# HGRN states with the heads of a pair taking turns on TensorE, a finer order of its steps, and the output stage's first loads in the joining stage

## The chip, the core and the metric

One core of a Trainium2 chip runs the whole kernel. Its engines are TensorE (PE, its weight loads are shown apart as PEld), VectorE (DVE), ScalarE (ACT), GpSimd (POOL) and SyncE (SP), which here only issues transfers. The metric is the device time of one launch in microseconds (us). The kernel before takes 4038.7 us (median of three runs, 4037.71 to 4042.99).

## The reference

One layer of a two-branch sequence mixer with an MLP, on 2048 latent tokens and 256 context tokens of width 1024, all in float32:

```python
h = modulate(rms_norm(x), shift, scale)
p = h @ w_in                        # columns for both head groups
oa = gated_delta(p)                 # 8 heads of 64, forward and backward summed
ob = hgrn2(p)                       # 8 heads of 64, tokens in column-major order of a 32 x 64 grid
ya = head_rms(oa, gdn_g) * silu(ga)
yb = from_col_major(head_rms(ob, hgrn_g)) * sigmoid(gb)
x = x + gate1 * (concat(ya, yb) @ w_out)
x = x + gate2 * (relu(modulate(rms_norm(x)) @ w1) ** 2 @ w2)
out = rms_norm(x)
```

HGRN2 in chunks: each chunk of 128 tokens has a state S (64 x 64 for each head and direction), S_t = f_t S_(t-1) + delta_t, and the output of a chunk is q_dec @ S of the chunk ahead of it, plus what comes from inside the chunk.

## The kernel before

The program is a row of stages with a barrier between them: `phase_front`, `phase_project`, `phase_gdn` (the delta heads), `phase_hgrn` (context, chunks, states), `phase_merge` and `phase_out`. The change touches the last three: the states, the joining stage and the output stage.

**`phase_hgrn_states`.** The chunk stage has left in SBUF, for each of the 16 chunks and 8 heads, the state increment `e.delta` (both directions, one in each half of the partitions), and the part of the output from inside the chunks, `e.oi`. In DRAM lie the decayed queries `e.sqd` (2 MB for a pair of heads) and the gates `e.sgb`. The stage works on four pairs of heads, `a`:

- `scan` (DVE, L2242): the recurrence over 16 chunks, one instruction for a head and chunk, each waiting by `scanned` for the one of the chunk before. It runs in two halves of four heads (`HB` = 4): `scan(0)` ahead of all, `scan(1)` behind `add(0)`.
- `order(h)` (ACT, L2207 and L2208): copies a head's states into `st`, two instructions; `st` holds four heads.
- `outputs(a)` (PE, L2170): for each head of the pair 16 products of the states (128 x 64) with 128 columns of queries, head 0 into partitions 0 to 63 of PSUM `ps`, then head 1 into partitions 64 to 127. It waits for the pair's queries (`q_in`), for `o_sum` of the pair before (`ps` is single) and for `ordered`.
- `add(a)` (DVE, L2250) sums `ps` and `e.oi` into `o`, `square(a)` (ACT, L2214) squares it, `sums(a)` (PE, L2179) sums over the head's channels, `roots(a)` (ACT, L2220) and `inverse(a)` (DVE, L2254, a reciprocal) give one factor for each token and head in `rt`, `spreads(a)` (PE, L2189, four blocks of 512 tokens) spreads it over the partitions into one of three buffers `bc`, and `scale(a)` (DVE, L2264, four blocks) multiplies. `gate` (POOL for the first three pairs, DVE for the last, L2153) multiplies by the gate, and the result is stored to `e.sy`.
- The SP queue, in order: queries and gates of pairs 0 and 1; for pair 2 a wait for `outputs(0)`, its queries, a wait for `gate(0)`, its gates, the store of pair 0; for pair 3 the same, one pair on. So the queries of pair 3 stand behind the wait for `gate(0)` and behind the gates of pair 2 and the store of pair 0.

Orders of the engines in this stage, written out by hand: PE outputs 0, outputs 1, sums 0, spreads 0, sums 1, spreads 1, outputs 3 and so on (with outputs 2 behind spreads 0); DVE scan 0, add 0, scan 1, inverse 0, add 1, scale 0, inverse 1, add 2 and so on; ACT order 0 to 3, square 0, order 4 and 5, roots 0, square 1, order 6 and 7, roots 1.

**`phase_merge`** joins the two directions of the delta heads, in four blocks `b` of 512 tokens with two sets of buffers: three loads of 1 MB (`y_of`, `y_ob`, `y_ga`), an add, squares, sums, roots, a scaling, 64 small transposing products, the gate, and a store to `e.sy`. The loads of block 2 wait until block 0 is through.

**`phase_out`** runs 288 units of 24 matmuls (128 x 128 by 128 x 512; each operand is split in a high and a low part, hence three products for each of 8 input tiles `k`). Units 0 to 7 are the output projection of block 0, 8 to 15 that of block 1, then the MLP. The weights of a unit (512 KB) go into one of two buffers `raw`, are split by ACT (`o_w_hi`, L2600) and DVE (`o_w_lo`, L2679) and used by PE (L2559 to L2561). The SP queue begins: weights 0, the joined input `yraw` of block 0 in four parts, weights 1, the residual `x1` of block 0 (2 MB), weights 2, `yraw` of block 1 (2 MB, behind the wait that all 8 tiles of block 0 are split), `x1` of block 1 (2 MB), weights 3, weights 4 and so on.

Of the kernel before, what the change touches and what calls it, by code (L numbers as in the profile page):

```python
# [28 lines left out]
P = 128  # L29
D = 1024  # L30
KT = D // P
# [2072 lines left out]
def phase_hgrn_states(nc, e):  # L2104

    NS = NC2 + NL2
    with ExitStack() as ctx:
# [19 lines left out]
        with nc.Block() as block:  # L2127
            @block.sync
            def _(sp):
                sp.dma_start(pick[:, :], e.consts[:, K_PICK, 0:NB * HEADS]).then_inc(const_in, 16)  # L2130
                sp.dma_start(spread[:, :, :], e.consts[0:HEADS, K_SPREAD:K_SPREAD + NB, :]).then_inc(const_in, 16)
                for a in range(PAIRS):
                    if a >= 2:
                        sp.wait_ge(full, 2 * (a - 1))
                    sp.dma_start(qd[:, a % 2], e.sqd[:, 2 * a:2 * a + 2, :]).then_inc(q_in[a % 2], 16)
                    if a >= 2:
                        sp.wait_ge(gated, a - 1)
                    sp.dma_start(gb[:, a % 2], e.sgb[a]).then_inc(g_in[a % 2], 16)
                    if a >= 2:
                        sp.dma_start(e.sy[PAIRS + a - 2], yb[:, a % 2]).then_inc(stored[a % 2], 16)  # L2140
                for a in range(PAIRS - 2, PAIRS):
                    if a == PAIRS - 1:
                        sp.wait_ge(gated_last, 1)
                    else:
                        sp.wait_ge(gated, a + 1)
                    sp.dma_start(e.sy[PAIRS + a], yb[:, a % 2]).then_inc(stored[a % 2], 16)
                for p in range(2):
                    sp.wait_ge(stored[p], 32)
# [12 lines left out]
            def _(pe):  # L2161
                def outputs(a):
# [3 lines left out]
                    for x in range(2):  # L2166
                        h = 2 * a + x
                        pe.wait_ge(ordered, 2 * (h + 1))
                        for c in range(NL2):
                            last = nc.tensor.matmul(ps[x * HD:x * HD + HD, c * C2:(c + 1) * C2], st[:, h % 4, c, :],  # L2170
                                                    qd[:, a % 2, x, c * C2:(c + 1) * C2], start=True, stop=True)
                        last.then_inc(full, 1)
# [19 lines left out]
                outputs(0)  # L2192
                for a in range(PAIRS):
                    if a == 0:
                        outputs(1)
                    sums(a)
                    spreads(a)
                    if 0 < a + 2 < PAIRS:
                        outputs(a + 2)

            @block.scalar
            def _(act):
                def order(h):
                    act.wait_ge(scanned, NL2 * HB * (h // HB) + (NL2 - 1) * HB + h % HB + 1)
                    if h >= 4:
                        act.wait_ge(full, h - 3)
# [20 lines left out]
                for a in range(PAIRS):  # L2227
                    square(a)
                    if a + 2 < PAIRS:
                        order(2 * a + 4)  # L2230
                        order(2 * a + 5)
                    roots(a)

            @block.vector
            def _(dve):
                def scan(g):
                    for t in range(1, 1 + NL2):
                        for x in range(HB):
                            h = HB * g + x
                            if t >= 2:  # L2240
                                dve.wait_ge(scanned, NL2 * HB * g + (t - 2) * HB + x + 1)
# [3 lines left out]
                def add(a):  # L2245
                    dve.wait_ge(full, 2 * (a + 1))
# [22 lines left out]
                scan(0)  # L2269
                for a in range(PAIRS):  # L2270
                    add(a)
                    if a == 0:
                        scan(1)
                    if a:
                        scale(a - 1)
                    inverse(a)
                scale(PAIRS - 1)
# [13 lines left out]
def phase_merge(nc, e):  # L2291

    G = TB // CH
    with ExitStack() as ctx:
# [12 lines left out]
        stored = [sem("y_st0"), sem("y_st1")]  # L2307
        added, squared, summed, root, inv, scaled, turned, gated = (
            sem("y_" + n) for n in ("add", "sq", "sum", "root", "inv", "scaled", "turned", "gated"))
        with nc.Block() as block:  # L2310
            @block.sync
            def _(sp):
                for b in range(NB):
# [6 lines left out]
                    sp.dma_start(ga[:, p], e.sga[:, :, b * TB:(b + 1) * TB].rearrange("a p t -> p a t")).then_inc(load[p], 16)  # L2320

# [53 lines left out]
def phase_out(nc, e):  # L2375

    FC = FF // D
    with ExitStack() as ctx:
# [9 lines left out]
        x1 = sb("o_x1", [P, 2, KT, TB])  # L2388
        yraw = sb("o_yraw", [P, KT, TB])
        raw = sb("o_raw", [P, 2, KT, P])  # L2390
# [8 lines left out]
        w_in, x_in, out_st = ([sem(n + "0"), sem(n + "1")] for n in ("w_in", "x_in", "out_st"))  # L2399
        y_in = [sem("y_in%d" % i) for i in range(4)]  # L2400
# [7 lines left out]

        units = []
# [61 lines left out]
        with nc.Block() as block:  # L2471
            @block.sync
            def _(sp):
# [8 lines left out]
                def y_load(b):  # L2482
                    if b:
                        sp.wait_ge(y_lo_ready, KT * b)
                    for i in range(4):
# [12 lines left out]

                weights(0)
                y_load(0)  # L2500
                weights(1)
                x_load(0)
# [37 lines left out]
            def _(pe):  # L2540
                def unit(i):
# [8 lines left out]
                    for k in range(KT):  # L2550
                        if s == 0:
                            if kind == "o":
                                pe.wait_ge(y_lo_ready, KT * b + k + 1)
# [5 lines left out]
                        nc.tensor.matmul(out, w_hi[:, i % 2, k, :], rhs[0][:, k, :], start=(k == 0), stop=False)  # L2559
                        nc.tensor.matmul(out, w_hi[:, i % 2, k, :], rhs[1][:, k, :], start=False, stop=False)  # L2560
                        last = nc.tensor.matmul(out, w_lo[:, i % 2, k, :], rhs[0][:, k, :], start=False, stop=(k == KT - 1))  # L2561
# [33 lines left out]
            def _(act):  # L2595
# [58 lines left out]
                for k in range(KT):  # L2654
# [21 lines left out]
            def _(dve):  # L2676
# [4 lines left out]
                def y_split(b, k):  # L2681
                    hi, lo = y_pair(b)
                    dve.wait_ge(y_hi_ready, KT * b + k + 1)
# [46 lines left out]
                for k in range(KT):  # L2730
                    y_split(0, k)
                for i in range(LAST):
# [20 lines left out]
                    if at_step(i, KT + 2) is not None:  # L2753
                        inverse(at_step(i, KT + 2))


def program(nc, a):
# [7 lines left out]
    with ExitStack() as ctx:  # L2765
# [37 lines left out]
        phase_merge(nc, e)  # L2803
        phase_out(nc, e)

# [17 lines left out]
```

## Time and profile before

| | |
|---|---|
| median of three runs | 4038.7 us |
| the profiled execution | 4046.5 us |
| its span, first to last instruction | 4044.7 us |
| PE busy | 3591.9 us (89%) |
| DVE, ACT, POOL busy | 45%, 38%, 22% |
| granted TensorE clock, mean | 0.925 |
| HGRN states | 2203.6 to 2327.7 us |
| joining stage | 2332.1 to 2419.0 us |
| output stage | 2419.4 us to the end |

The profile shows one execution. "Busy" is time in which an engine executes; the idle time ahead of an instruction is shown in brackets with what ended it. A row of a timeline gives start, duration and instruction; xN means N instructions in one row. A granted clock of 1.00 is TensorE at 2.4 GHz, 0.50 at 1.2 GHz. A stage is read from its own stretch of the trace, since the averages over the span mix stages with different limits.

### The profile page before, as it was taken

What the parts mean: (1) busy time and instruction counts of PE and PEld (TensorE: products, weight loads), DVE (VectorE), ACT (ScalarE), POOL (GpSimd) and SP (SyncE); (2) the same over time, 40 slices, a digit from 0 to 9 for tenths busy, and PEclk for the clock granted to TensorE, in tenths of its full rate; (3) what the DMA queues carried; (4) which work ended last, traced back from release to release, by engine and by line L of the source; (5) the groups of instructions that cost most, each with busy time, mean ns of one, the idle gap of its engine ahead of it and who ended that gap; (6) DMA issues with size and microseconds to landing.
All of it is one profiled execution on the core that took longest, in us unless ns stands there. A gap on an engine that the chain in (4) does not pass through costs nothing. (4 is left out here: it accounts for less than half of the span.)

```text
span 4044.7 us, 98792 instructions
## 1 busy us (share of the span) xinstructions
PE 3591.9 (89%) x42320; PEld 2982.7 (74%) x42320; DVE 1824.9 (45%) x2710; ACT 1526.2 (38%) x2048; POOL 894.5 (22%) x872
## 2 busy tenths in 40 slices
PE   6899999999788888858776729999999999999999
PEld 3677888888577777747666427888888888888887
DVE  5488302110155555545555545444543454435443
ACT  5566324432255555413334113333422343234223
POOL 0220233320245555325553102000100110011001
PEclk8899999999799999956776769999999999999999
DMA  6233434442233333243332255333343333333332
GB/s 250 76 82 60 97 101 141 136 138 66 88 109 104 108 105 109 87 117 97 97 84 86 94 196 158 115 99 117 108 124 99 94 115 116 98 98 111 99 95 88
DMA packets 599111, 441.14 MB, mean 109 GB/s; under 512 B 119948, under 2 KB 548304, under 8 KB 591576
## 3 DMA queue, kind: packets, MB, share of 16 engines
q1 hardware_dynamic: 574048, 408.20, 34.7%
q0 software_dynamic: 5632, 16.78, 1.4%
q10 hardware_dynamic: 19192, 12.65, 1.1%
q8 instruction: 190, 3.11, 0.3%
q14 instruction: 49, 0.40, 0.0%
HBM read 338.17 MB, written 99.39 MB: 108 GB/s over the span
## 5 line engine op out<-in xcount | busy, mean ns | idle before, releaser
L618 PE MATMUL p_pg<-h_hi,p_whi 128*128 128x512 f32 (+1 forms) x1384 | 531.3, 384 | 10.0 <-DVE p_wlo L847 10.0
L2600 ACT ACTIVATE o_w_hi<-o_raw 128x1024 fp32r<-128x1024 f32 x288 | 303.6, 1054 | 590.6 <-PE o_pg L2561 551.8
L618 PE MATMUL p_pg<-h_hi,p_wlo 128*128 128x512 f32 (+1 forms) x1384 | 519.2, 375 | 0.0
L618 PE MATMUL p_pg<-h_lo,p_whi 128*128 128x512 f32 (+1 forms) x1384 | 519.2, 375 | 0.0
L2559 PE MATMUL o_pg<-o_f_hi,o_w_hi 128*128 128x512 f32 x1088 | 424.8, 390 | 0.0
L2561 PE MATMUL o_pg<-o_f_hi,o_w_lo 128*128 128x512 f32 x1088 | 423.3, 389 | 0.0
L2560 PE MATMUL o_pg<-o_f_lo,o_w_hi 128*128 128x512 f32 x1088 | 423.3, 389 | 0.0
L2559 PE MATMUL o_pg<-o_h_hi,o_w_hi 128*128 128x512 f32 x1024 | 400.0, 391 | 1.7 <-DVE o_w_lo L2679 1.7
L2561 PE MATMUL o_pg<-o_h_hi,o_w_lo 128*128 128x512 f32 x1024 | 398.5, 389 | 0.0
L2560 PE MATMUL o_pg<-o_h_lo,o_w_hi 128*128 128x512 f32 x1024 | 398.4, 389 | 0.0
L2679 DVE TENSOR_TENSOR o_w_lo<-o_raw,o_w_hi 128x1024 fp32r<-128x1024 f32 x288 | 351.4, 1220 | 77.4 <-ACT o_w_hi L2600 77.3
L2534 POOL COPY o_rt<-o_sq 128x512 f32<-128x512 f32 x8 | 9.2, 1151 | 1389.2 <-ACT o_sq L2614 1389.2
L618 PEld LDWEIGHTS p_pg<-h_hi,p_whi 128*128 128x128 f32 x1384 | 262.4, 190 | 61.5 <-DVE p_wlo L847 10.3
L618 PEld LDWEIGHTS p_pg<-h_lo,p_whi 128*128 128x128 f32 x1384 | 262.3, 190 | 51.2 <-issue 5.5
L2695 DVE SCALAR_TENSOR_TENSOR o_x<-o_pg,mod,o_x 128x512 f32<-128x512 f32 x160 | 119.9, 750 | 397.3 <-PE o_pg L2561 392.7
L618 PEld LDWEIGHTS p_pg<-h_hi,p_wlo 128*128 128x128 f32 x1384 | 262.0, 189 | 46.9
L2701 DVE TENSOR_TENSOR o_rl<-o_rl 128x512 f32<-128x512 f32 x128 | 88.7, 693 | 393.8 <-ACT o_f_hi L2640 393.8
L2638 ACT ACTIVATE o_rl<-o_pg 128x512 f32<-128x512 f32 x128 | 76.5, 598 | 430.3 <-PE o_pg L2561 430.3
L2559 PEld LDWEIGHTS o_pg<-o_f_hi,o_w_hi 128*128 128x128 f32 x1088 | 204.2, 188 | 43.4 <-issue 0.7
L2560 PEld LDWEIGHTS o_pg<-o_f_lo,o_w_hi 128*128 128x128 f32 x1088 | 204.3, 188 | 42.8 <-issue 0.7
L2561 PEld LDWEIGHTS o_pg<-o_f_hi,o_w_lo 128*128 128x128 f32 x1088 | 204.2, 188 | 42.5
L826 ACT ACTIVATE p_y<-p_pg 128x512 f32<-128x512 f32 (+1 forms) x108 | 97.0, 898 | 361.1 <-PE p_pg L618 245.3
(310 smaller groups left out, 6909.6 us busy)
## 6 DMA issues: line engine op xcount, KB each, us to landing
o_raw<-in_w_mlp SPq DMA_DIRECT2D x256, 512.0 KB, 4.1
g_kqvb<-scr_kqv SPq DMA_DIRECT2D x72, 384.0 KB, 3.4
p_raw<-in_w_in SPq DMA_DIRECT2D x38, 512.0 KB, 5.9
g_kqa<-scr_kqv SPq DMA_DIRECT2D x72, 256.0 KB, 3.1
p_mw<-in_w_mod POOLq DMA_DIRECT2D x64, 256.0 KB, 3.1
o_raw<-in_w_out SPq DMA_DIRECT2D x32, 512.0 KB, 4.1
scr_kqv<-p_y SPq DMA_DIRECT2D x24, 576.0 KB, 5.7
scr_hf<-p_y SPq DMA_DIRECT2D x16, 576.0 KB, 5.5
```

The source lines that it names most:

```text
L618: last = nc.tensor.matmul(pg[0:m, bank, 0:n], w[:, q, k, 0:m], h[bank][:, k, :], start=(k == 0 and j == 0), stop=(k == KT - 1 and j == 2))
L826: last = nc.scalar.activation(put(yrow[u]), src, f)
L2534: nc.gpsimd.tensor_copy(rt[:, c % 3, :], sq[:, n % 3, :]).then_inc(sq_used, 1)
L2559: nc.tensor.matmul(out, w_hi[:, i % 2, k, :], rhs[0][:, k, :], start=(k == 0), stop=False)
L2560: nc.tensor.matmul(out, w_hi[:, i % 2, k, :], rhs[1][:, k, :], start=False, stop=False)
L2561: last = nc.tensor.matmul(out, w_lo[:, i % 2, k, :], rhs[0][:, k, :], start=False, stop=(k == KT - 1))
L2600: nc.scalar.activation(w_hi[:, i % 2], raw[:, i % 2], ACT.Copy).then_inc(w_hi_ready, 1)
L2638: nc.scalar.activation(rl[:, n % 3, :], pg[:, i % 4, :], ACT.Relu).then_inc(rectified, 1)
L2679: dve.tensor_tensor(w_lo[:, i % 2], raw[:, i % 2], w_hi[:, i % 2].bitcast(F32), ALU.subtract).then_inc(w_lo_ready, 1)
L2695: dve.scalar_tensor_tensor(x, pg[:, i % 4, :], e.mod[:, gate:gate + 1], x, ALU.mult, ALU.add).then_inc(added, 1)
L2701: dve.tensor_tensor(rl[:, n % 3, :], rl[:, n % 3, :], rl[:, n % 3, :], ALU.mult).then_inc(f_sq, 1)
```

## The change

In the states: `outputs(a)` now waits for both heads of the pair and issues, chunk by chunk, the product of head 0 and then that of head 1; `full` counts pairs. `scan` runs in four parts of two heads. The orders become: PE outputs 0, outputs 1, sums 0, outputs 2, spreads 0, sums 1, outputs 3, spreads 1, sums 2, sums 3, spreads 2, spreads 3; DVE scan 0, scan 1, add 0, scan 2, add 1, inverse 0, scan 3, scale 0, add 2, inverse 1, scale 1, add 3, inverse 2, scale 2, inverse 3, scale 3; ACT order 0 to 3, square 0, order 4 and 5, roots 0, square 1, order 6 and 7, roots 1, square 2 and so on. The SP queue keeps its order; its waits on `full` are recounted.

In the joining stage, SP issues behind the loads of block 1 also weights 0 and 1 of the output stage, the second half of `yraw` of block 0 (the HGRN part, 1 MB) and its `x1` (2 MB), 4 MB in all. The output stage then loads only the first half of `yraw` of block 0 ahead of weights 2, and takes the tiles of block 0 in the order 4 to 7, 0 to 3 (`FIRST`), in unit order, in the splits and in the waits. The buffers and semaphores of these loads are made in a new function around both stages. Left out below: the allocations that move there, and one of two alike loops over `FIRST`.

```diff
@@ -2131,7 +2131,7 @@
...
                     if a >= 2:
-                        sp.wait_ge(full, 2 * (a - 1))
+                        sp.wait_ge(full, a - 1)
@@ -2163,13 +2163,12 @@
...
                         pe.wait_ge(o_sum, a)
-                    for x in range(2):
-                        h = 2 * a + x
-                        pe.wait_ge(ordered, 2 * (h + 1))
-                        for c in range(NL2):
-                            last = nc.tensor.matmul(ps[x * HD:x * HD + HD, c * C2:(c + 1) * C2], st[:, h % 4, c, :],
+                    pe.wait_ge(ordered, 4 * (a + 1))
+                    for c in range(NL2):
+                        for x in range(2):
+                            last = nc.tensor.matmul(ps[x * HD:x * HD + HD, c * C2:(c + 1) * C2], st[:, (2 * a + x) % 4, c, :],
                                                     qd[:, a % 2, x, c * C2:(c + 1) * C2], start=True, stop=True)
-                        last.then_inc(full, 1)
+                    last.then_inc(full, 1)
@@ -2190,20 +2189,23 @@
...
                 outputs(0)
+                outputs(1)
+                sums(0)
                 for a in range(PAIRS):
-                    if a == 0:
-                        outputs(1)
-                    sums(a)
+                    if a + 2 < PAIRS:
+                        outputs(a + 2)
+                    if a + 2 >= PAIRS and a + 1 < PAIRS:
+                        sums(a + 1)
                     spreads(a)
-                    if 0 < a + 2 < PAIRS:
-                        outputs(a + 2)
+                    if a + 2 < PAIRS:
+                        sums(a + 1)
...
                 def order(h):
-                    act.wait_ge(scanned, NL2 * HB * (h // HB) + (NL2 - 1) * HB + h % HB + 1)
+                    act.wait_ge(scanned, 2 * NL2 * (h // 2 + 1) - 1 + h % 2)
                     if h >= 4:
-                        act.wait_ge(full, h - 3)
+                        act.wait_ge(full, h // 2 - 1)
@@ -2224,26 +2226,33 @@
...
                     order(h)
-                for a in range(PAIRS):
-                    square(a)
-                    if a + 2 < PAIRS:
-                        order(2 * a + 4)
-                        order(2 * a + 5)
-                    roots(a)
+                square(0)
+                order(4)
+                order(5)
+                roots(0)
+                square(1)
+                order(6)
+                order(7)
+                for a in range(1, PAIRS):
+                    if a + 1 < PAIRS:
+                        roots(a)
+                        square(a + 1)
+                    else:
+                        roots(a)
...
             def _(dve):
-                def scan(g):
+                def scan(a):
                     for t in range(1, 1 + NL2):
-                        for x in range(HB):
-                            h = HB * g + x
+                        for x in range(2):
+                            h = 2 * a + x
                             if t >= 2:
-                                dve.wait_ge(scanned, NL2 * HB * g + (t - 2) * HB + x + 1)
+                                dve.wait_ge(scanned, 2 * (NL2 * a + t - 2) + x + 1)
...
                 def add(a):
-                    dve.wait_ge(full, 2 * (a + 1))
+                    dve.wait_ge(full, a + 1)
@@ -2267,14 +2276,18 @@
...
                 scan(0)
+                scan(1)
+                add(0)
+                scan(2)
+                add(1)
+                inverse(0)
+                scan(3)
                 for a in range(PAIRS):
-                    add(a)
-                    if a == 0:
-                        scan(1)
-                    if a:
-                        scale(a - 1)
-                    inverse(a)
-                scale(PAIRS - 1)
+                    scale(a)
+                    if a + 2 < PAIRS:
+                        add(a + 2)
+                    if a + 1 < PAIRS:
+                        inverse(a + 1)
@@ -2305,6 +2318,7 @@
...
         stored = [sem("y_st0"), sem("y_st1")]
+        wo = e.w_out[0]
@@ -2318,6 +2332,13 @@
...
                     sp.dma_start(ga[:, p], e.sga[:, :, b * TB:(b + 1) * TB].rearrange("a p t -> p a t")).then_inc(load[p], 16)
+                    if b == 1:
+                        for i in range(2):
+                            sp.dma_start(e.o_raw[:, i], wo[:, i * P:(i + 1) * P].rearrange("(k p) c -> p k c", p=P)).then_inc(e.o_w_in[i], 16)
+                        for i in range(PAIRS // 2, PAIRS):
+                            sp.dma_start(e.o_yraw[:, 2 * i:2 * i + 2], e.sy[2 * i:2 * i + 2, :, 0:TB].rearrange("k p t -> p k t")
+                                         ).then_inc(e.o_y_in[i], 16)
+                        sp.dma_start(e.o_x1[:, 0], e.xT[:, :, 0:TB].rearrange("k p t -> p k t")).then_inc(e.o_x_in[0], 16)
@@ -2406,6 +2425,7 @@
...
+        FIRST = [*range(PAIRS, KT), *range(PAIRS)]
@@ -2479,10 +2499,10 @@
...
-                def y_load(b):
+                def y_load(b, quarters=range(4)):
...
                         sp.wait_ge(y_lo_ready, KT * b)
-                    for i in range(4):
+                    for i in quarters:
@@ -2496,10 +2516,7 @@
...
-                weights(0)
-                y_load(0)
-                weights(1)
-                x_load(0)
+                y_load(0, (0, 1))
@@ -2547,18 +2564,18 @@
...
                             pe.wait_ge(added, add_no[i - 3])
-                    for k in range(KT):
+                    for n, k in enumerate(FIRST if kind == "o" and b == 0 else range(KT)):
...
                             if kind == "o":
-                                pe.wait_ge(y_lo_ready, KT * b + k + 1)
+                                pe.wait_ge(y_lo_ready, KT * b + n + 1)
...
                         out = pg[:, i % 4, :]
-                        nc.tensor.matmul(out, w_hi[:, i % 2, k, :], rhs[0][:, k, :], start=(k == 0), stop=False)
+                        nc.tensor.matmul(out, w_hi[:, i % 2, k, :], rhs[0][:, k, :], start=(n == 0), stop=False)
                         nc.tensor.matmul(out, w_hi[:, i % 2, k, :], rhs[1][:, k, :], start=False, stop=False)
-                        last = nc.tensor.matmul(out, w_lo[:, i % 2, k, :], rhs[0][:, k, :], start=False, stop=(k == KT - 1))
+                        last = nc.tensor.matmul(out, w_lo[:, i % 2, k, :], rhs[0][:, k, :], start=False, stop=(n == KT - 1))
@@ -2651,7 +2668,7 @@
...
                 split(0)
-                for k in range(KT):
+                for k in FIRST:
@@ -2727,7 +2744,7 @@
...
                 split(0)
-                for k in range(KT):
+                for k in FIRST:
@@ -2754,6 +2771,20 @@
...
+def phase_tail(nc, e):
+    with ExitStack() as ctx:
+        def sem(n):
+            return ctx.enter_context(nc.semaphore("o_" + n))
...
+        e.o_x1 = ctx.enter_context(nc.sbuf_tensor("o_x1", [P, 2, KT, TB], F32))
+        e.o_yraw = ctx.enter_context(nc.sbuf_tensor("o_yraw", [P, KT, TB], F32))
+        e.o_raw = ctx.enter_context(nc.sbuf_tensor("o_raw", [P, 2, KT, P], F32))
+        e.o_w_in, e.o_x_in = ([sem(n + "0"), sem(n + "1")] for n in ("w_in", "x_in"))
+        e.o_y_in = [sem("y_in%d" % i) for i in range(4)]
+        phase_merge(nc, e)
+        phase_out(nc, e)
@@ -2800,9 +2831,8 @@
...
         phase_hgrn(nc, e)
-        phase_merge(nc, e)
-        phase_out(nc, e)
...
+        phase_tail(nc, e)
```

## Rows read from the trace of the kernel before

**Rows 1.** Stretches: us, busy PE, PEld, DVE, ACT, POOL (xcount), clock, DMA share, GB/s

```profile
2203.50:2327.80 124.30, 81.88 (x320) 48.52 (x320) 66.87 (x153) 28.46 (x26) 13.50 (x3) 0.68 0.33 127
...
2462.00:4044.00 1582.00, 1571.97 (x6986) 1300.17 (x6984) 722.58 (x818) 529.51 (x690) 99.38 (x61) 1.00 0.36 104
```

**Rows 2.** Timeline, first part of the HGRN states: start, duration, instruction, idle before

```profile
2203.59 12.62 DVE L2242 SCALAR_TENSOR_TENSOR h_delta<-h_delta,s_gs 128x64 f32<-128x64 f32 x64 [1.96 <-ACT s_gs L2224]
...
2215.66 1.06 ACT L2207 ACTIVATE s_st<-h_delta 64x1024 f32<-64x1024 f32 x1 [12.10 <-DVE h_delta L2242]
...
2217.94 9.31 PE L2170 MATMUL s_ps<-s_qd,s_st 128*64 128x128 f32 x64 [17.75 <-ACT s_st L2208]
...
2245.86 1.28 ACT L2220 ACT_TABLE_LOAD   x1
...
2247.87 3.34 DVE L2254 RECIPROCAL s_rt<-s_rt 8x512 f32<-8x512 f32 x1 [5.76 <-ACT s_rt L2220]
```

**Rows 3.** Timeline, last two pairs of the HGRN states

```profile
2282.76 9.35 PE L2170 MATMUL s_ps<-s_qd,s_st 128*64 128x128 f32 x64
...
2284.03 4.50 POOL L2153 TENSOR_TENSOR s_yb<-s_yb,s_gb 128x2048 f32<-128x2048 f32 x1 [19.86 <-DVE s_yb L2264]
...
2292.03 3.60 PE L2179 MATMUL s_pn<-s_sq,s_pick 128*8 128x512 f32 x8
...
2301.90 1.91 ACT L2214 ACTIVATE s_sq<-s_o 128x2048 f32<-128x2048 f32 x1 [5.55 <-DVE s_o L2250]
2303.59 1.07 DVE L2264 SCALAR_TENSOR_TENSOR s_yb<-s_o,cols,s_bc 128x512 f32<-128x512 f32 x1 [0.60 <-PE s_bc L2189]
...
2325.42 2.29 DVE L2153 TENSOR_TENSOR s_yb<-s_yb,s_gb 128x2048 f32<-128x2048 f32 x1
```

**Rows 4.** One line's instructions in a short stretch: count, ns min/median/max, first and last start

```profile
L2170 PE MATMUL s_ps<-s_qd,s_st x16: 421/421/421, 2218.6 to 2221.8; 128*64 128x128 f32 x16
...
L2170 PE MATMUL s_ps<-s_qd,s_st x12: 272/273/273, 2225.8 to 2227.0; 128*64 128x128 f32 x12
...
L1868 PE MATMUL b_py<-b_vt,b_kdt x32: 222/222/271, 2199.0 to 2200.0; 128*64 128x64 f32 x32
```

**Rows 5.** A stretch inside the first output products: the granted clock

```profile
2220.00:2225.00 5.00, 5.00 (x37) 5.00 (x36) 0.00 (x0) 4.19 (x4) 0.00 (x0) 0.69 0.00 0
```

**Rows 6.** DMA issues of 2203.60, 2265.05, 2362.08, 2426.21, 2438.15: size, us to landing

```profile
s_qd<-scr_qd SPq DMA_DIRECT2D x1, 2048.0 KB, 7.2
...
s_qd<-scr_qd SPq DMA_DIRECT2D x1, 2048.0 KB, 13.9
...
y_ga<-scr_ga SPq DMA_DIRECT2D x1, 1024.0 KB, 14.5
...
o_raw<-in_w_out SPq DMA_DIRECT2D x1, 512.0 KB, 13.7
...
o_raw<-in_w_out SPq DMA_DIRECT2D x1, 512.0 KB, 14.3
```

**Rows 7.** Timeline: third block's loads and add in the joining stage, and the output stage's start

```profile
2362.08 4.52 SPq L2320 DMA_DIRECT2D y_ga<-scr_ga  x1
...
2378.04 2.28 DVE L2358 TENSOR_TENSOR y_of<-y_of,y_ob 128x2048 f32<-128x2048 f32 x1
...
2423.88 1.06 ACT L2600 ACTIVATE o_w_hi<-o_raw 128x1024 fp32r<-128x1024 f32 x1 [20.27 <-DMA o_raw<-in_w_out]
2424.96 1.22 DVE L2679 TENSOR_TENSOR o_w_lo<-o_raw,o_w_hi 128x1024 fp32r<-128x1024 f32 x1 [10.23 <-ACT o_w_hi L2600]
...
2426.94 0.76 PE L2559 MATMUL o_pg<-o_y_hi,o_w_hi 128*128 128x512 f32 x1 [14.61 <-DVE o_y_lo L2684]
...
2431.49 5.37 SPq L2486 DMA_DIRECT2D o_yraw<-scr_y  x4
...
2438.15 32.45 SPq L2480 DMA_DIRECT2D o_raw<-in_w_out  x6
...
2454.84 0.29 PEld L2559 LDWEIGHTS o_pg<-o_y_hi,o_w_hi 128*128 128x128 f32 x1 [7.21 <-DVE o_w_lo L2679]
```

More of the change, by code:

```diff
@@ L2387, in phase_out @@
         y_hi, y_lo = sb("o_y_hi", [P, KT, TB], F32R), sb("o_y_lo", [P, KT, TB], F32R)
-        x1 = sb("o_x1", [P, 2, KT, TB])
-        yraw = sb("o_yraw", [P, KT, TB])
-        raw = sb("o_raw", [P, 2, KT, P])
+        x1, yraw, raw = e.o_x1, e.o_yraw, e.o_raw
         w_hi, w_lo = sb("o_w_hi", [P, 2, KT, P], F32R), sb("o_w_lo", [P, 2, KT, P], F32R)
@@ L2398, in phase_out @@
         pt = ctx.enter_context(nc.psum_tensor("o_pt", [P, 2, TB], F32))
-        w_in, x_in, out_st = ([sem(n + "0"), sem(n + "1")] for n in ("w_in", "x_in", "out_st"))
-        y_in = [sem("y_in%d" % i) for i in range(4)]
+        w_in, x_in, y_in = e.o_w_in, e.o_x_in, e.o_y_in
+        out_st = [sem("out_st0"), sem("out_st1")]
         w_hi_ready, w_lo_ready, product = sem("w_hi"), sem("w_lo"), sem("product")
@@ L2682, in y_split @@
                     hi, lo = y_pair(b)
-                    dve.wait_ge(y_hi_ready, KT * b + k + 1)
+                    dve.wait_ge(y_hi_ready, KT * b + (FIRST.index(k) if b == 0 else k) + 1)
                     dve.tensor_tensor(lo[:, k, :], yraw[:, k, :], hi[:, k, :].bitcast(F32), ALU.subtract).then_inc(y_lo_ready, 1)
```

## The prediction

> **What bounds the kernel now.** I read the stretches of the span first, then the timeline of the states and of the output stage's start, then single lines and transfers. From 2462 us on TensorE is busy for 1572 of 1582 us at the full clock [rows 1]: nothing that the change does there can gain, and what comes earlier simply moves that block. Ahead of it stand the 124 us of the states, where TensorE is busy for 82 us at a mean clock of 0.68 and VectorE for 67 us [rows 1]. Neither is full: the stage is one dependent chain. The reader is to see in the timeline that the first product waits 17.75 us for the scan and the copies of the states, and that the first reciprocal starts only at 2247.87, behind a whole second scan [rows 2]; later a pair costs about 24 us of products, sums, roots, reciprocal, spreading and scaling, one behind another [rows 3]. The output stage starts empty: its first matmul comes at 2426.94, 7.5 us after the first issue at 2419.4, and the fourth unit's weights let TensorE wait 7.21 us until 2454.84 [rows 7].
>
> **Turns on TensorE.** The same 64 instructions for a pair stay. Head after head they start 0.213 us apart at the low clock (16 from 2218.6 to 2221.8) and 0.109 us at the full one (12 from 2225.8 to 2227.0) [rows 4]. The nearest row for turns is the chunk stage's line 1868, which alternates its output between the same two halves: 32 instructions of 64 columns in 1.0 us, 0.032 us each, where 64 columns at 0.109 us for 128 would take 0.055 [rows 4]. That is a ratio of 1.7 with the rounding of the starts; it cannot pass 2 with two halves. Ends: ratio 1 (no gain) and 2. I take 2, since 31 steps in about 0.95 us fit it. A pair is then 0.107 us a step at the low clock, 0.055 at the full one. The clock in the first group was low until about 2223.1 (0.69 of 5 us is 3.1 us low) [rows 5], 5.2 us after its start. With the same 5.2 us, 48 steps run low and 16 full: 5.2 + 0.9 + 0.2 for the last to end is 6.2 us, against 9.31 [rows 2].
>
> The Trainium skill speaks against this part: "TensorE: Matmul & The Clock Gate", the part on packing small matmuls, says that a weight load overlaps matmuls in flight only where the row group differs, and turns between two halves of columns keep the row group. The line 1868 disagrees as far as it goes. What this would give is worked out below, as a rival.
>
> **The states, walked through.** Scan steps start 12.62/64 = 0.197 us apart, so a quarter (32 steps) takes 6.3 us [rows 2]. A new step waits for the one two before it instead of four; two steps are 0.39 us, one instruction lasts 0.28, so 0.197 stays; the other end, a step waiting out 0.28 + 0.04 each time, is 0.32 (an estimate, bounded above by those durations).
> - Scan 0 to 2209.9. Four copies at 1.08 [rows 2] to 2214.1. The queries landed 7.2 us after 2203.60, at 2210.8 [rows 6], in time. Outputs 0 to 2220.3 (before: 2227.3).
> - Add 0, 2.2 us (taken like the other 128x2048 operation, 2.28 [rows 7]), to 2222.5; scan 2 to 2228.9; copies of pair 2 to 2233.1; table load and roots 2.0 (2245.86 to 2247.87 [rows 2]) to 2235.1; reciprocal 3.3 to 2238.4; scan 3 to 2244.7; scale 0, four blocks of 1.09, to 2249.1. Outputs 1, outputs 2, sums 0, add 1 and three of the four spreads lie beside this. Waiting outputs 2 would hold up spreads 0 in PE's queue, but they end at 2239.2, before spreads 0 can matter under scan 3.
> - Here a wait appears. The queries of pair 3 are issued behind gate 0 (4.5 us on POOL [rows 3]) and two more issues: 2249.1 + 4.5 + 0.9 = 2254.5. Together with that store and those gates they took 13.9 us to land [rows 6], in time before, since they were issued at 2265.05 and needed at 2282.76 [rows 3]. Now they land at 2268.4, while TensorE has ended sums 1 at 2253.8. Outputs 3 stand ahead of spreads 1 and sums 2 in its queue, so VectorE, done with reciprocal 1 at 2257.9, waits too, over 16 us.
> - Outputs 3 from a low clock, 6.1 us, to 2274.5; spreads 1 and scale 1, 5.3 us, to 2279.8; add 3 to 2282.1; beside it sums 2 at the low clock (6.2) to 2284.0; roots 2 and square 3 (0.7, from the 2.0 less the 1.28 of the table load [rows 2], and 1.9 [rows 3]) to 2286.7; sums 3 (3.6 [rows 3]) to 2290.3; spreads 2 and scale 2 to 2295.6; reciprocal 3 to 2298.9; spreads 3 and scale 3 at the low clock, first block 1.9, then a pitch of 1.07 + 0.60 [rows 3], to 2307.2; gate 2.3 [rows 3] to 2309.5.
>
> The same walk with the old orders and durations gives 2327.5, where the trace has 2327.7. The states so gain 18.2 us. With landings of 10 us instead of 13.9 the walk gives 22; with the clock rising 3.4 to 5.7 us after the start of a group it gives 15 to 23.
>
> **The joining stage.** Added: 4 MB behind the 6 MB of blocks 0 and 1, on the queue that next loads block 2. A 2 MB load on an idle queue took 7.2 us [rows 6], and a full queue moved 4.7 million bytes in 12.55 us (next part), 376 GB/s; so some 2 us pass before data flow, and the 10.5 million bytes issued from 2332 on end near 2362 to 2364. Block 2's issues come at 2361 and their data begin to flow 2 us later, so they lose 0 to 1.5 us. Their last one is issued at 2362.08, took 14.5 us [rows 6], landed at 2376.6 and is needed at 2378.04 [rows 7]: 1.4 us of cover. Cost 0, at most 3 if small packets move slower; with the cover gone every microsecond counts. The five issues themselves are done by then, as SP has nothing else to do until 2361.
>
> **The output stage.** At 2419.4 weights 0 and the upper half of the input are there. Split 1.06 + 1.22 [rows 7] to 2421.8, the first tile's low part 0.65 later: first matmul at 2422.5 instead of 2426.94. The other four tiles land by about 2424.7 and are split by 2427.0, each before its turn, as a tile takes 3 x 0.43 at the low clock. Now the input of block 1 can be issued at 2427.0 instead of 2431.49 [rows 7], and on an empty queue: before, the residual and weights 2 were still ahead of it until 2426.21 + 13.7 = 2439.9 [rows 6]. From there to the landing of weights 3 at 2438.15 + 14.3 = 2452.45 [rows 6, 7] it was 12.55 us for the same 4.5 MB. So weights 3 land at 2427.0 + 2 + 12.55 = 2441.6, and with the two splits the fourth unit starts at 2443.9 instead of 2454.84 [rows 7]: 10.9 us. Units 0 to 2 (7.2, 5.4, 5.4 us) end at 2440.5, so its wait is 3.4 us. If the clock no longer falls in it, 2 more are gained. I take 11. From the fourth unit on it is the dense block, moved as a whole.
>
> **The sum.** 18 + 0 + 11 = 29 us. The profiled execution (span 4044.7, time 4046.5) would take 4017.5; its median stands 7.8 us lower, at 4038.7, so the forecast is 4009.7.
>
> **The rivals.**
> - Turns give nothing: the change doesn't do what it says, the two heads only swap places in the same row of instructions. The pair costs the old 9.3 us; the walk ends at 2316.4, a gain of 11.3 in the states and 22 in all: 4016.4. Against it is line 1868. Chance 0.10. This is also how it would go by the rule of the Trainium skill cited above.
> - The granted clock stays at 0.50 through the states, since the groups of products are shorter and end before it rose in the first group. Each pair's sums, spreads and products are then low: the walk gives 2324.1, 3.6 us gained and 14.6 in all: 4024. For it: the mean of 0.68 [rows 1] already. Chance 0.11. The other way, if it is mostly high, the walk gives 2299 to 2302: about 4001. Chance 0.09.
> - The scan in two chains instead of four runs at 0.32 us a step: the walk gives 2321.1; 17.6 in all: 4021. Chance 0.07.
> - The extra 4 MB make block 2's loads late by 5 us and more: 4015 to 4019. Chance 0.04.
> - Two or more of the losing cases meet: 4031 to 4039. Chance 0.04.
> - Slower: the scan again. Every step hangs on the one just two before it; if release and refill make a step 0.7 us (2.5 times its 0.28), the walk ends 41.6 us later than before, and with 11 from the output stage the kernel takes 4069. It decides from about 0.6 us a step, where the loss passes the 11 us by 0.2% of the time; nothing in the rows is near. Chance 0.02.
>
> **How the numbers follow.** The forecast case has 0.53 and by itself spans 4003 to 4017. The range takes in the clock and scan rivals: 4000 to 4024, leaving out the slower case and the far ends. About 0.2% (8 us) is what a measurement of this kernel tells from no change. Faster by more than that 0.94, within it 0.04 (the case where losses meet), slower 0.02.
>
> **What would show it.** In the states of after: product groups of 3.5 to 6.5 us; the scan at 0.197; a wait of TensorE ahead of the fourth group for the queries' transfer, ending near 19 us earlier than the whole stage's old schedule would have it (2268); stage end near 2309. In the joining stage: no wait of the third block's add. In the output stage: first matmul about 3 us after its first issue, one wait of 3 to 4 us ahead of the fourth unit. The prediction falls if the fourth group isn't held by its queries (more gain) or if products, scan or clock show the rivals' figures.

## The result, and the profile after

The changed kernel takes 4010.9 us (median of 4 runs, 4006.7 to 4014.2) beside 4038.2 for the kernel before (4 runs): 0.9931 of it, 95% interval 0.9913 to 0.9948. The forecast was 4009.7, range 4000 to 4024. A second measurement, on another occasion, gave 4019.5 (6 runs, 3997.2 to 4029.3) beside 4037.0, a ratio of 0.9939 (0.9918 to 0.9959). The gain is there both times, but its size is less sure than one interval says: the two medians of the first measurement lie 27.3 us apart, those of the second only 17.5 (a ratio here is not the quotient of the two medians). Single runs spread widely; the last section comes back to it.

The profiled execution has a span of 4004.9 us, 39.8 less than before. That overstates the change: its HGRN states start at 2194.2 and not at 2203.6, 9.4 us earlier, behind code that is the same in both. So all comparisons below count from the first query transfer of the states, which leaves out what an execution gains or loses ahead of them. All values are us. The forecast of 29 and the 30.4 of the last row lie closer together than their parts, and that is luck: this profile is 4.1 better than forecast in the states and 3.0 worse ahead of the fourth unit. The second profile of the same kernel has 23.7 in the last row.

| | before | after | difference | forecast |
|---|---|---|---|---|
| HGRN states, first query transfer to the last gate's end | 124.1 | 101.8 | -22.3 | -18.2 |
| joining stage, first issue to the output stage's first issue | 87.4 | 87.0 | -0.4 | 0 |
| output stage's first issue to its first matmul | 7.5 | 3.1 | -4.4 | -4.4 |
| first issue to the fourth unit | 35.4 | 27.5 | -7.9 | -10.9 |
| first issue to the end of the span | 1625.3 | 1617.5 | -7.8 | |
| start of the states to the end of the span | 1841.1 | 1810.7 | -30.4 | -29 |

The whole stretch of the states, which answers to [rows 1] (us, busy PE, PEld, DVE, ACT, POOL, granted clock, DMA share, GB/s):

```profile
2194.20:2296.10 101.90, 56.88 (x320) 29.77 (x320) 65.45 (x153) 28.18 (x25) 13.54 (x3) 0.72 0.41 155
```

TensorE is busy 25 us less for the same 320 instructions; VectorE's 65 us are nearly as before (67) and now fill 64% of the stage. The timeline of the states after, with the steps that carry the walk, answers to [rows 2, 3] (start, duration, instruction, idle before):

```profile
2204.80 6.59 PE L2169 MATMUL s_ps<-s_qd,s_st 128*64 128x128 f32 x64 [14.03 <-ACT s_st L2210]
...
2224.26 3.72 PE L2169 MATMUL s_ps<-s_qd,s_st 128*64 128x128 f32 x64 [1.52 <-ACT s_st L2210]
...
2226.14 3.34 DVE L2263 RECIPROCAL s_rt<-s_rt 8x512 f32<-8x512 f32 x1 [3.95 <-ACT s_rt L2222]
...
2245.40 0.43 SPq L2135 DMA_DIRECT2D s_qd<-scr_qd  x1
2258.66 5.30 PE L2169 MATMUL s_ps<-s_qd,s_st 128*64 128x128 f32 x64 [15.00 <-DMA s_qd<-scr_qd]
2263.89 3.70 PE L2188 MATMUL s_bc<-s_rt,s_spread 8*128 8x512 f32 x8
2265.05 3.81 DVE L2273 SCALAR_TENSOR_TENSOR s_yb<-s_o,cols,s_bc 128x512 f32<-128x512 f32 x4 [17.30 <-PE s_bc L2188]
2267.52 3.60 PE L2178 MATMUL s_pn<-s_sq,s_pick 128*8 128x512 f32 x8
...
2285.39 7.19 PE L2188 MATMUL s_bc<-s_rt,s_spread 8*128 8x512 f32 x8 [4.48 <-DVE s_rt L2263]
```

The first products come 10.6 us after the stage's start (14.3 before) and last 6.59 instead of 9.31. The first reciprocal starts 32.0 us in, where it was 44.3. And there is the new wait of the forecast: TensorE idle for 15.00 us for the fourth pair's queries, VectorE for 17.30 behind it.

The output stage's start, against [rows 7]:

```profile
2387.36 0.88 SPq L2506 DMA_DIRECT2D o_yraw<-scr_y  x2
2387.38 1.06 ACT L2617 ACTIVATE o_w_hi<-o_raw 128x1024 fp32r<-128x1024 f32 x1 [15.15 <-PEq L2324]
...
2390.44 0.77 PE L2576 MATMUL o_pg<-o_y_hi,o_w_hi 128*128 128x512 f32 x1 [10.16 <-DVE o_y_lo L2701]
...
2394.98 3.41 SPq L2506 DMA_DIRECT2D o_yraw<-scr_y  x4
...
2398.95 68.06 SPq L2500 DMA_DIRECT2D o_raw<-in_w_out  x12
...
2414.84 0.79 PE L2576 MATMUL o_pg<-o_y_hi,o_w_hi 128*128 128x512 f32 x1 [5.65 <-DVE o_w_lo L2696]
```

The wait ahead of the third unit is gone, that of the fourth is 5.65 us. The third unit's wait before was this:

```profile
2442.28 0.50 PE L2559 MATMUL o_pg<-o_y_hi,o_w_hi 128*128 128x512 f32 x1 [2.15 <-DVE o_w_lo L2679]
```

### The profile page after: what moved, and what is told of

It reads as the page before. It is cut to its first block and busy times, and to the rows that moved or that the text cites. A ratio compares the mean times of both kernels' runs of the same rounds, so it can differ in the third digit from the quotient of the medians.

```text
span 4004.9 us, 98792 instructions
## 1 busy us (share of the span) xinstructions
PE 3555.6 (89%) x42320; PEld 2953.1 (74%) x42320; DVE 1824.9 (46%) x2710; ACT 1525.3 (38%) x2048; POOL 891.0 (22%) x872
```

## The experiments

Each kernel has two results: its time, as a ratio to the kernel before with its interval, and the stage lengths of its profile. A single time carries the luck of the 2190 us ahead, so where the question is one stage, the stage length decides: by their times alone the changed kernel, the one without turns (0.9943) and the one with the scan in halves (0.9951) can't be told apart, as their intervals overlap. The states of the old code took 124.1 us both in the kernel before and in the second experiment below. The new ones took 101.8, 104.4, 105.5 and 108.7 in four kernels with the same states; so a difference of a few us between two single profiles of the new states is read from its steps, not from the sum.

### Only the states

Everything behind the states is the kernel before's.

> Only the HGRN states are changed; the joining and output stages are those of before. Theory (three independent parts): the states last 101.8 us as in the changed kernel against 124.1 before, the joining stage 87.4 and the first 35.4 us of the output stage stay, so about 22 us less than before, 4016. Rival (part of the gain is made by the other stages or given back in them): the states do not fall to 102, or the joining stage grows by what they gave.

Measured: 0.9958 (0.9943 to 0.9973), some 17 us. States 105.5, joining stage 87.1, first issue to the fourth unit 35.8; from the start of the states 1823.6, 17.5 less than before. The other stages take no part in the gain and give back 1.1. The states' gain is 18.6, four less than in the changed kernel, though the code is the same; 22 was expected.

### Only the early transfers

The states are the kernel before's, the rest is the changed kernel's.

> Only the early transfers and the tile order are changed; the states are those of before. Theory: the joining stage stays at 87 us, the fourth unit's first matmul comes 27.5 us after the output stage's first issue instead of 35.4, 8 us less than before, 4030. Rival (the 4 MB collide with the third block's loads when nothing else has changed ahead of them): the third block's add waits for its loads and the gain is 5 or less.

Measured: 0.9986 (0.9974 to 0.9999), some 6 us. States 124.1, joining stage 87.3, first issue to the fourth unit 26.8; from the start of the states 1833.5, 7.6 less. The 4 MB cost nothing in the joining stage here either. 17.5 and 7.6 make 25.1; the changed kernel's two profiles (30.4 and 23.7) and its two time ratios (27.9 and 24.6 us of 4038) lie on both sides of the sum. What the early transfers and what the order of the tiles give was not taken apart.

### The turns taken back

```diff
-                    for c in range(NL2):
-                        for x in range(2):
+                    for x in range(2):
+                        for c in range(NL2):
```

> The changed kernel, but the products of head 0 all stand ahead of those of head 1 again. Theory (turns halve the time of a pair's products): each pair's group lasts 8.4 to 9.4 us instead of 3.7 to 6.6; on the chain stand the first and the fourth group, so the states last about 6 us longer, 108. Rival (the two heads do not overlap, the group is short for another reason such as the clock): groups and stage stay as they are, 101.8.

Measured: 0.9943 (0.9924 to 0.9961); states 112.6. Groups at the full clock throughout are the clean comparison: the second one here, the third one in the changed kernel (count, ns min/median/max, first and last start):

```profile
L2169 PE MATMUL s_ps<-s_qd,s_st x64: 272/273/323, 2211.4 to 2217.9; 128*64 128x128 f32 x64
```

```profile
L2169 PE MATMUL s_ps<-s_qd,s_st x64: 272/273/324, 2224.3 to 2227.7; 128*64 128x128 f32 x64
```

63 steps in 6.5 us are 0.103 each, 63 in 3.4 are 0.054. The single instruction lasts 0.273 in both kernels and only their starts move together: with turns they follow 1.9 times as fast, so the instructions of two heads do overlap more. On the chain stand the first group (8.1 against 6.6) and the fourth (9.5 against 5.3), together 5.7 us, the 6 expected. Most of the other 5 are steps that ran in part at the low clock here and not there (sums of the third and fourth pair 6.3 and 5.3 against 3.6 each). The rival is out.

### The turns alone

The kernel before with chunk by chunk products of both heads, nothing else.

> The kernel before with the turns alone; all orders, the scan in halves and the transfers are the old ones. Theory: groups of 4 to 6.6 us; the first also waits 2.1 us longer for the second head's copies, so it gives 0.5, the third and fourth stand between scale and sums on the chain and give some 3 to 4 each, so the states last about 116 to 117 instead of 124.1. Rival (groups become so short that the clock never rises in them, so sums and spreads run at the low clock): 120 or more.

Measured: 0.9982 (0.9967 to 0.9997), about 7 us; states 116.9, 7.2 less. The first group now starts 2.2 us later, for the second head's copies, and lasts 6.55; the third and fourth last 6.5 and 6.1 instead of 9.6 and 9.4:

```profile
2209.51 6.55 PE L2169 MATMUL s_ps<-s_qd,s_st 128*64 128x128 f32 x64 [19.91 <-ACT s_st L2208]
...
2240.10 7.19 PE L2189 MATMUL s_bc<-s_rt,s_spread 8*128 8x512 f32 x8 [12.68 <-DVE s_rt L2254]
2247.22 6.47 PE L2169 MATMUL s_ps<-s_qd,s_st 128*64 128x128 f32 x64
2253.62 3.60 PE L2179 MATMUL s_pn<-s_sq,s_pick 128*8 128x512 f32 x8
```

The sums behind them still take 3.60: the granted clock is 0.50 in the first half of the third group, 0.61 in the second and 1.00 in its sums, so it rose before the shorter group ended, and the rival is out. So of the change's states the turns are worth some 7 us alone, and inside the new order 4 to 6: 5.7 by the groups on the chain, 3.9 against the changed kernel's slower profile (108.7).

### The fourth pair's queries early

```diff
                 for a in range(PAIRS):
-                    if a >= 2:
-                        sp.wait_ge(full, a - 1)
-                    sp.dma_start(qd[:, a % 2], e.sqd[:, 2 * a:2 * a + 2, :]).then_inc(q_in[a % 2], 16)
+                    if a < 2:
+                        sp.dma_start(qd[:, a % 2], e.sqd[:, 2 * a:2 * a + 2, :]).then_inc(q_in[a % 2], 16)
+                    if a == 2:
+                        for n in (2, 3):
+                            sp.wait_ge(full, n - 1)
+                            sp.dma_start(qd[:, n % 2], e.sqd[:, 2 * n:2 * n + 2, :]).then_inc(q_in[n % 2], 16)
                     if a >= 2:
                         sp.wait_ge(gated, a - 1)
```

> The changed kernel, but the queries of the fourth pair are issued right behind those of the third, ahead of the wait for the first gate. Theory (the queue holds the fourth pair's products, and all behind them, for some 15 us): no wait for that transfer, spreads of the second pair start 16 us earlier, the states last 86 us instead of 101.8. Rival (VectorE's and the reciprocal's chain is next and close behind, so the wait was hiding another): 95 or more.

Measured: 0.9881 (0.9862 to 0.9901), states 88.2: 13.6 less than the changed kernel's 101.8, and more against its other executions. The timeline of TensorE shows the wait gone:

```profile
2246.92 4.87 PE L2181 MATMUL s_pn<-s_sq,s_pick 128*8 128x512 f32 x8
2251.72 3.71 PE L2172 MATMUL s_ps<-s_qd,s_st 128*64 128x128 f32 x64
2255.93 3.70 PE L2191 MATMUL s_bc<-s_rt,s_spread 8*128 8x512 f32 x8 [0.50 <-DVE s_rt L2266]
2259.56 5.30 PE L2181 MATMUL s_pn<-s_sq,s_pick 128*8 128x512 f32 x8
```

The second pair's spreads start 53.4 us into the stage instead of 69.7, the 16 us expected; 2.7 are given back in the sums (5.30 against 3.60) and the third spreads (4.82 against 3.70), which begin at the low clock here. The wait hid no other of its size: by the place of one transfer in SP's queue the change leaves 13.6 us, more than half of what it gained in the states.

### The scan in halves again

Four heads a part, order scan 0, add 0, scan 1, add 1, inverse 0, all else as in the changed kernel.

> The changed kernel with the scan in two halves of four heads again, the second half behind the first add; orders of the products stay. Theory (the quarter lets the first products start 6 us earlier, and the third pair's copies): the first product starts 16.4 us after the scan instead of 10.6, the first scale ends near 53 us instead of 45.8, the states last about 109. Rival (the wait for the fourth pair's queries hangs on POOL's first gate and swallows nothing, or other waits take it up): 102 to 105.

Measured: 0.9951 (0.9931 to 0.9971); states 115.0. The front is as expected: first products 16.5 us in, first scale to 52.6 us. The fourth group starts 72.0 us in instead of 64.5, so the 7 us of the front pass through the queries' wait undiminished, since their issue hangs on the first gate. The rest of the 13 us (the fourth group to the end takes 43.0 instead of 37.3) is the clock again: the sums take 5.8 and 5.0 where they took 3.6, and the changed kernel's second profile takes 43.8 for the same stretch. So the quarters are worth about 7 us, as much as the turns. What the new order of the products and scalings gives by itself was not run.

### Weights ahead of the second block's input

```diff
-                    if i == 0:
-                        y_load(1)
-                        x_load(1)
+                    if i == 1:
+                        y_load(1)
+                    if i == 2:
+                        x_load(1)
```

> The changed kernel, but the output stage issues the fourth unit's weights ahead of the second block's input, and the fifth's ahead of its residual. Theory (the fourth unit waits only because 4 MB stand ahead of its weights): its wait of 5.65 us goes, and with it the low clock behind it, some 2 us: 7 to 8 us less than the changed kernel. Rival (the transfers are at their full rate, so the wait moves to the fifth or sixth unit): a wait of 2 to 4 us there, and 2 to 4 gained.

Measured: 0.9922 (0.9900 to 0.9945); states 104.4. TensorE has no wait at all in the first 60 us behind its first matmul, and the output stage takes 1609.5 us from its first issue instead of 1617.5: 8.0 us, the 5.65 of the wait and the low clock behind it. The wait did not move on to a later unit, so the rival is out.

### TensorE's last idle time filled

```diff
+                    if a == PAIRS - 1:
+                        pe.wait_ge(o_sum, PAIRS)
+                        for c in range(NL2):
+                            for x in range(2):
+                                nc.tensor.matmul(ps[x * HD:x * HD + HD, c * C2:(c + 1) * C2], st[:, (2 * a + x) % 4, c, :],
+                                                 qd[:, a % 2, x, c * C2:(c + 1) * C2], start=True, stop=True)
                     spreads(a)
```

> The changed kernel with the fourth pair's products done a second time, to no use, behind the third spreads, in the 4.5 us in which TensorE waits for the last reciprocal. Theory (that idle time lets the clock fall and the last spreads run at 0.50): the last eight spreads take 3.7 us instead of 7.2, the last four scalings go without a pause, the states last 3 us less. Rival (spreads of 8 rows run at the low clock whatever is ahead, or the filling delays them): no change or 1 us longer.

Measured: 0.9919 (0.9893 to 0.9946); states 98.4, 3.4 less than 101.8, with the third spreads ending at the same place (86.5 and 86.7 us in):

```profile
2280.03 3.71 PE L2203 MATMUL s_ps<-s_qd,s_st 128*64 128x128 f32 x64
2284.66 3.69 PE L2188 MATMUL s_bc<-s_rt,s_spread 8*128 8x512 f32 x8 [0.92 <-DVE s_rt L2269]
```

Work to no use makes the stage shorter: the last spreads take 3.69 us instead of 7.19, at a granted clock of 1.00 instead of 0.50. The clock's fall in an idle time of 4.5 us is what the last part paid for. The time of this kernel has a second gain in it that the filling didn't make: its fourth unit in the output stage waited 3.52 us instead of 5.65 and that stage took 1614.2 instead of 1617.5, with the same code.

### Both waits taken away, and the changed kernel beside them

These three ran on one chip in one go: the early queries with the weights first; the same with the idle time filled; the changed kernel again.

> The changed kernel with the fourth pair's queries early and the output stage's weights ahead of the second block's input, both together. Theory (two independent waits): the states last 88 us and the output stage counts 1609.5 us from its first issue, 8 less; from the start of the states to the end 1789 us instead of 1810.7, so some 21 us under the changed kernel, 3989. Rival (the gains meet in the transfers or are lost to the clock): less than 15 us.

> The same, and the fourth pair's products once more, to no use, in TensorE's wait for the last reciprocal. Theory: the last spreads run at the full clock here too, 3.4 us less than without, the states 85 us, 3986. Rival (with the earlier queries TensorE does less ahead of this wait, so the clock is low there already when the filling starts): the filling runs at 0.50 and ends late, no gain, or up to 2 us lost.

> The changed kernel again, beside the two others on the same chip. Theory: the states 102 to 105 us by the clock's luck, the joining stage 87, 27.5 us from the output stage's first issue to the fourth unit; 0.993 of the kernel before. Rival (the first measurement caught lucky executions): 0.995 or more.

| | median | ratio to before | 95% interval | states | start of the states to the end |
|---|---|---|---|---|---|
| both | 3987.6 | 0.9884 | 0.9865 to 0.9902 | 91.1 | 1791.3 |
| both, filled | 3984.5 | 0.9871 | 0.9856 to 0.9887 | 89.1 | 1789.3 |
| changed again | 4019.5 | 0.9939 | 0.9918 to 0.9959 | 108.7 | 1817.4 |

"Both" is 19.4 us under the changed kernel's first profile from the start of the states on and 26 under its second, where the two single gains make 21.6: the two waits are independent. The filling gives 2.0 here instead of 3.4. The spreads fall from 7.2 to 3.7 us, but the filling, begun at the low clock, takes 5.80 us and holds them back 1.3 us: theory and rival each hold in part. The filled one has the lowest median of all, but its interval overlaps that of "both", so it isn't shown to be faster. The third row shows how much the clock does to the same code. The stretch of its states:

```profile
2210.10:2318.90 108.80, 63.18 (x320) 31.43 (x320) 65.70 (x153) 28.18 (x25) 13.52 (x3) 0.67 0.39 145
```

The same 320 instructions keep TensorE 6.3 us longer, at 0.67 instead of 0.72, and the stage is 6.9 us longer; VectorE's time is unchanged. Only 0.4 of the 6.9 us lie ahead of the fourth group, whose queries landed that much later.

## Why the prediction was right, and where it was not

**Turns.** The ratio was taken as 2 between ends of 1 and 2, from line 1868 of [rows 4]. It is 1.9 (0.054 us a step against 0.103). The first group took 6.59 us, forecast 6.2. The rule of the Trainium skill ("TensorE: Matmul & The Clock Gate", on packing small matmuls), that weight loads overlap matmuls in flight only with another row group, does not hold here: these turns share the row group and still start 0.054 us apart, each with a weight load of its own, which lasts 0.137:

```profile
L2169 PEld LDWEIGHTS s_ps<-s_qd,s_st x64: 133/137/138, 2224.2 to 2227.6; 128*64 128x64 f32 x64
```

**The walk through the states.** Counted from the stage's start, forecast and measured: first products 10.5 and 10.6; first reciprocal 31.5 and 32.0; first scale's start 41.1 and 41.4; queries issued 50.9 and 51.2; fourth group 64.8 and 64.5. The scan kept its pitch with two chains: 32 steps in 6.34 us, less the last one's 0.28, are 0.195 a step.

```profile
2213.64 6.34 DVE L2251 SCALAR_TENSOR_TENSOR h_delta<-h_delta,s_gs 128x64 f32<-128x64 f32 x32
```

The new wait was foreseen with its cause and its length, and the early queries show both. Behind it the forecast and the first profile part: 2.6 us by the sums of the third pair, taken at the low clock, 6.2, and measured at 3.60, and 0.8 by the fourth group; the last spreads start 91.2 us in, forecast 95.3. With the second profile the same steps went the other way, to 108.7 in all against 105.9. So the size was right for the middle of what the stage does, 101.8 to 108.7 in four profiles, and the clock rival, which was given 0.11 for low throughout and 0.09 for mostly high, was wrong in form: the third and fourth pair's sums met either level, another one from profile to profile, and that moved the stage over 7 us. One reading in the prediction was a slip: the fourth group was to start not "near 19 us earlier" but 14.4 (2282.76 to 2268.4); it came 14.7 earlier, counted from the stage's start.

**The joining stage.** Cost 0 was right: no add waited for its loads, here or in the kernel with the early transfers alone. The cover was 3.2 us and not 1.4: the third block's loads, issued at 2331.32, took 13.3 us to land, at 2344.6, for an add at 2347.87, which stood 1.5 us later in the stage than before.

```profile
y_ga<-scr_ga SPq DMA_DIRECT2D x1, 1024.0 KB, 13.3
...
2347.87 2.28 DVE L2379 TENSOR_TENSOR y_of<-y_of,y_ob 128x2048 f32<-128x2048 f32 x1
```

**The output stage.** The first matmul came 3.1 us in, as forecast. The term that was mis-sized is the landing of weights 3. The issue of the second block's input came 7.6 us in, as forecast. From there to the landing I took 2 us and then the 12.55 us of a full queue, 14.55; it took 17.5 (2394.98 to 2398.95 + 13.5). The stretches of 2 us from there on show why:

```profile
2395.36:2397.36 2.00, 2.00 (x10) 1.62 (x10) 0.99 (x1) 0.00 (x0) 0.00 (x0) 1.00 0.56 154
2397.36:2399.36 2.00, 2.00 (x11) 1.65 (x10) 0.75 (x1) 0.95 (x1) 0.00 (x0) 1.00 0.85 214
2399.36:2401.36 2.00, 2.00 (x11) 1.65 (x10) 1.86 (x2) 1.67 (x4) 1.15 (x1) 1.00 0.89 303
2401.36:2403.36 2.00, 2.00 (x10) 1.66 (x9) 0.99 (x2) 0.00 (x0) 0.00 (x0) 1.00 1.01 356
```

154, 214 and 303 GB/s in the last column: the queue was empty when the loads were issued, and SP needed 3.4 us for the first four, so the rate of a full queue (376 GB/s, the prediction's 4.7 million bytes in 12.55 us) was not reached for 6 us, and the 2 us set aside for that were too few. The price taken from a queue with work waiting in it didn't hold for the same bytes on an idle one. That is 3 of the 10.9 us. It is 3 in this profile: with the same code the landing took 15.6 to 17.8 us in seven profiles, and 15.6 where SP issued the four in 1.9 us. How much of the slow start is the issuing and how much the transfers' own was not tested. Over all profiles the fourth unit started 35.4 to 36.5 us after the first issue with the old code and 25.3 to 27.8 with the new, 8.9 less on average, so the term was 2 too large. The weights-first kernel shows the same place from the other side: with the 512 KB ahead of the 4 MB nothing waits.

The forecast of 29 us thus has a states term of 18 that lies inside what was measured (15.4 to 22.3), an output term that is 2 to 3 too large, and a sum (25.1 by the two halves alone, 24.6 and 27.9 by the ratios) that is some 1 to 4 us smaller than forecast.

## What to carry to other kernels

When a chain is shortened, look at each transfer that hangs on its end by the order of a queue: its issue moves less than its use. Here the fourth pair's queries waited for a gate that they had no need of, and moving one issue was worth 13.6 us, more than the turns or the finer scan. Where products write different halves of the partitions, try taking them in turn: here it cost no instruction and took a group at the full clock from 6.8 to 3.7 us. Its price is that the first group waits for the operands of both halves, 2.2 us here.

## What the runs showed of the hardware that was not expected

The granted clock goes with unequal times of equal code, and more than the trace of one execution lets one guess. The chunk stage ahead of the states is the same in all 13 kernels here. From its first load to the first query transfer of the states it took from 429.1 to 445.4 us. In the six shortest profiles (429.1 to 429.4) its granted clock was 0.70 to 0.72, in the two longest, only the states and the changed kernel again, 0.66 and 0.64. First a short one, the turns taken back, then only the states, in the same stretch of the span (us, busy PE, clock, DMA share, GB/s):

```profile
1845.00:2185.00 340.00, 254.84 (x8587) 0.73 0.34 82
```

```profile
1845.00:2185.00 340.00, 267.38 (x8283) 0.65 0.33 80
```

Between these ends the order is loose: the fourth pair's queries early had the highest clock of all (0.73) and took 433.3. The kernel with the turns taken back starts its states at 2190.2 us, that with only the states changed at 2213.0: 23 us between executions of the same instructions, nearly the size of the whole change, 16 of them in this stage and 7 ahead of it. That the clock is the cause, and not only goes with it, was not tested. For the states the steps themselves show it: the same sums take 3.60 us or 4.9 to 6.4 by the level they meet. And work to no use in an idle time of 4.5 us, just ahead of products on the chain, shortened the stage by 3.4 us.
